# A chunked RWKV-7 scan in 64x64 cells: another order of the work on four engines within a period

## The reference, cut to what matters

```python
def step(s, inp):
    r_t, w_t, k_t, v_t, a_t, b_t = inp
    sa = jnp.einsum('bhij,bhj->bhi', s, a_t)
    s = s * w_t[:, :, None, :] + sa[..., None] * b_t[:, :, None, :] + v_t[..., None] * k_t[:, :, None, :]
    return s, jnp.einsum('bhij,bhj->bhi', s, r_t)
```

## Time and profile before

| what | value |
|---|---|
| median of 3 runs | 2223.35 us (2222.14 to 2228.94) |
| the profiled execution, own time | 2223.72 us |
| its span, first to last instruction | 2221.9 us |
| mean granted clock of TensorE | 0.982 |
| TensorE matmul busy | 2041.6 us, 92% |
| VectorE busy | 1130.4 us, 51% |
| ScalarE busy | 646.0 us, 29% |
| GpSimd busy | 539.7 us, 24% |
| DMA | 248.23 MB, 36.0% of 16 engines' time |

### The profile page before, as it was taken

The page is one execution under the profiler, slowest core; times in us unless marked ns, Lnnn a source line. Parts: engine busy times, 40 slices in busy tenths (PEclk is TensorE's granted clock), DMA queues, the critical chain, the costliest instruction groups (busy, mean ns, idle before and its releaser), DMA issues. The chain is left out here.

```text
span 2221.9 us, 64762 instructions
## 1 busy us (share of the span) xinstructions
PE 2041.6 (92%) x28556; PEld 1325.2 (60%) x28556; DVE 1130.4 (51%) x2187; ACT 646.0 (29%) x1825; POOL 539.7 (24%) x669
## 2 busy tenths in 40 slices
PE   7999999999999999999896888888988898889698
PEld 3556565355444455544344777787878787878443
DVE  5443343134946670042624665665666666656574
ACT  4111111134255532210012332333333333333332
POOL 1010010023032410011122333333433333333011
PEclk9999999999999999999997999999999999999899
DMA  9201002701127765555413233523333323232732
GB/s 354 81 20 38 19 19 107 291 29 38 32 76 205 192 174 182 176 165 190 144 64 109 72 95 97 141 71 94 80 84 82 90 75 94 73 91 61 235 119 109
DMA packets 269818, 248.23 MB, mean 112 GB/s; under 512 B 92769, under 2 KB 226145, under 8 KB 266082
## 3 DMA queue, kind: packets, MB, share of 16 engines
q1 hardware_dynamic: 269538, 244.09, 36.0%
HBM read 164.32 MB, written 79.69 MB: 110 GB/s over the span
## 5 line engine op out<-in xcount | busy, mean ns | idle before, releaser
L2168 PE MATMUL ps<-M,NG 64*64 64x64 f32 x6400 | 258.3, 222 | 44.0 <-DVE M L2046 42.7
L1019 PE MATMUL ps<-xt,w_slab 128*128 128x512 f32 (+1 forms) x800 | 297.5, 525 | 0.0
L2168 PEld LDWEIGHTS ps<-M,NG 64*64 64x64 f32 x6400 | 221.9, 136 | 60.8 <-DVE M L2046 54.3
L1019 PEld LDWEIGHTS ps<-xt,w_slab 128*128 128x128 f32 x800 | 148.3, 190 | 146.3 <-issue 122.6
L2168 PE MATMUL ps<-TT,MT 64*64 64x64 f32 x5120 | 209.9, 220 | 5.9 <-issue 3.4
L2168 PEld LDWEIGHTS ps<-TT,MT 64*64 64x64 f32 x5120 | 179.4, 135 | 16.4 <-issue 6.4
L1895 POOL TENSOR_TENSOR SP<-S,decay 128x128 f32<-128x128 f32 x152 | 61.2, 403 | 518.8 <-DVE S L2080 503.4
L2071 DVE STREAM_TRANSPOSE MT<-M 128x256 f32<-128x256 f32 x240 | 106.0, 442 | 147.9 <-ACT M L1958 147.9
L1958 ACT ACTIVATE M<-ps 128x128 f32<-128x128 f32 x240 | 66.6, 278 | 353.7 <-PE ps L2168 353.7
L2029 DVE COPY_PREDICATED TT<-mask,ps 128x128 f32<-128x128 int32 x400 | 123.5, 309 | 54.5 <-PE ps L2168 45.0
L645 PE MATMUL ps<-h,fgo 128*128 128x512 f32 x320 | 141.6, 597 | 2.4 <-PEq L202 2.4
(11 more groups left out here) (298 smaller groups left out, 3996.7 us busy)
## 6 DMA issues: line engine op xcount, KB each, us to landing
feat<-feature_scratch SPq DMA_DIRECT2D x160, 256.0 KB
feature_scratch<-k_feats SPq DMA_DIRECT2D x64, 320.0 KB, 5.2
feature_scratch<-k_feats SPq DMA_DIRECT2D x24, 640.0 KB, 6.9
k_feats<-in_modw SPq DMA_DIRECT2D x8, 1536.0 KB, 6.6
w_slab<-in_rwin SPq DMA_DIRECT2D x24, 512.0 KB, 6.7
V<-v_token_scratch SPq DMA_DIRECT2D x320, 32.0 KB, 2.6
fgo<-in_modw SPq DMA_DIRECT2D x8, 1024.0 KB, 9.2
fw_slab<-in_fwin SPq DMA_DIRECT2D x16, 512.0 KB, 4.5
```

The costliest lines, as they stand in the source:

```text
L1019: mm = pe.matmul(ps[:, bank, 0:n], (w1t if i is None else w[:, i % 2])[:, k, :], src[:, k, a:a + n], start=k == 0, stop=k == KT - 1)
L2168: mm = pe.matmul(out[o, b, :], L[o, b, :], R[o, b, :], start=True, stop=True)
```

## The change

The same instructions are issued in another order in the `period` functions of GpSimd, ScalarE, VectorE and TensorE. On GpSimd the product into `ar` slot 0 is taken out of `operands` as `last_operand`, and the second `state_scaled` of the period now stands between the two. On TensorE `products(0)` and `m4` stand between `a_state(0)` and `r_state(0)`, `products(1)` ahead of `b_state(0)`, `y(0)` behind `m8`, and `y(1)` behind `t32`. On ScalarE `r(0)`, `first_n(0)`, `m4` and `sa(0)` stand ahead of the exponentials, and `sa(1)` ahead of `m16`. On VectorE `first_x(1)` is moved behind the first mask and transpose and behind t2, and the table `DA` follows that order. SyncE's list is the same.

```diff
--- before.py
+++ after.py
@@ -1682,7 +1682,7 @@
 PB = {"m4": 1, "t8": 2, "m8": 3, "t16": 4, "m16": 5, "t32": 6, "mt32": 7}
 AA = {"n0": 1, "n1": 2, "m2": 3}
 AB = {"m4": 1, "m8": 2, "m16": 3, "xt": 4}
-DA = {"x0": 1, "x1": 2, "mt1": 3, "m1": 4, "t2": 5, "mt2": 6, "t4": 7}
+DA = {"x0": 1, "mt1": 2, "m1": 3, "t2": 4, "x1": 5, "mt2": 6, "t4": 7}
 DB = {"mt4": 1, "t8": 2, "mt8": 3, "t16": 4, "mt16": 5, "t32": 6}
 
 LAT_ONLY = lambda n: [0, 0] + [n] * (NCH - 2)
@@ -1903,19 +1903,26 @@
                 for slot, lo in ((0, 128), (1, 0)):
                     g.tensor_tensor(d4(bk[s][:, :, slot, :]), fe(every, lo, 768), d4(E3[s][:]), ALU.mult).then_inc(op_ready, 1)
                 chunk_done(g, j, cc - SETS)
-                g.tensor_tensor(d4(ar[l][:, :, 0, :]), fe(every, 384, 256), before(cc, every), ALU.mult).then_inc(op_ready, 1)
+                if is_lat(cc):
+                    g.tensor_tensor(d4(ar[l][:, :, 2, :]), fe(every, 512, 640), upto(cc, every), ALU.mult).then_inc(op_ready, 1)
                 g.tensor_tensor(d4(ar[l][:, :, 1, :]), d4(ident.unsqueeze(1).broadcast_to([P, B4, CK])),
                                 pend(cc, every).unsqueeze(3).broadcast_to([P, 2, 2, CK]), ALU.mult).then_inc(op_ready, 1)
-                if is_lat(cc):
-                    g.tensor_tensor(d4(ar[l][:, :, 2, :]), fe(every, 512, 640), upto(cc, every), ALU.mult).then_inc(op_ready, 1)
+
+            def last_operand(j, cc):
+                s, l = par(cc), lng(cc)
+                every = slice(0, P)
+                g.tensor_tensor(d4(ar[l][:, :, 0, :]), F[s][:, 384:896].rearrange("p (d x) -> p d x", d=2)[:, :, 0:P].rearrange("p d (b t) -> p d b t", b=2), before(cc, every), ALU.mult).then_inc(op_ready, 1)
 
             def period(j, c, ahead):
+                coming = ahead or c + 3 < NCH
                 if c >= 0:
                     state_scaled(j, c, 0)
-                    if c < NCH - 1:
-                        state_scaled(j, c, 1)
-                if ahead or c + 3 < NCH:
+                if coming:
                     operands(j, c + 3)
+                if 0 <= c < NCH - 1:
+                    state_scaled(j, c, 1)
+                if coming:
+                    last_operand(j, c + 3)
 
             for j in range(KT):
                 for c in range(0 if j else -3, NCH):
@@ -1973,30 +1980,29 @@
 
             def period(j, c, ahead):
                 A_, B_, Q_ = c + 2 >= 0 and (ahead or c + 2 < NCH), c + 1 >= 0 and (ahead or c + 1 < NCH), c >= 0
+                if Q_:
+                    r(j, c, 0)
+                if A_:
+                    first_n(j, c + 2, 0)
                 if B_:
                     second(j, c + 1, "m4")
                 if Q_:
-                    r(j, c, 0)
+                    sa(j, c, 0)
                 if ahead or c + 3 < NCH:
                     exps(j, c + 3)
                 if j == 0 and c == -2:
                     identities(1)
                 if A_:
-                    first_n(j, c + 2, 0)
-                if Q_:
-                    sa(j, c, 0)
+                    first_n(j, c + 2, 1)
                 if B_:
                     second(j, c + 1, "m8")
-                if A_:
-                    first_n(j, c + 2, 1)
                 if Q_ and is_lat(c):
                     y(j, c, 0)
                 if Q_:
                     r(j, c, 1)
+                    sa(j, c, 1)
                 if B_:
                     second(j, c + 1, "m16")
-                if Q_:
-                    sa(j, c, 1)
                 if A_:
                     first_m2(j, c + 2)
                 if Q_ and is_lat(c):
@@ -2085,37 +2091,34 @@
                     cums(j, c + 3)
                 if j == 0 and c == -2:
                     masks()
+                if A_:
+                    first_x(j, c + 2, 0)
+                if A_ and is_lat(c + 2):
+                    first_r(j, c + 2, 0)
                 if B_:
                     second_mt(j, c + 1, 4)
-                if A_:
-                    first_x(j, c + 2, 0)
-                    if is_lat(c + 2):
-                        first_r(j, c + 2, 0)
-                if B_:
                     second_t(j, c + 1, 8)
                 if Q_:
                     state(j, c, 0)
-                if B_:
-                    second_mt(j, c + 1, 8)
                 if A_:
-                    first_x(j, c + 2, 1)
                     first_mt1(j, c + 2)
                     first_m1(j, c + 2)
                 if B_:
+                    second_mt(j, c + 1, 8)
                     second_t(j, c + 1, 16)
                 if A_:
-                    if is_lat(c + 2):
-                        first_r(j, c + 2, 1)
                     first_t(j, c + 2, 2)
+                    first_x(j, c + 2, 1)
+                if B_:
+                    second_mt(j, c + 1, 16)
+                if A_ and is_lat(c + 2):
+                    first_r(j, c + 2, 1)
                 if Q_:
                     state(j, c, 1)
                 if B_:
-                    second_mt(j, c + 1, 16)
+                    second_t(j, c + 1, 32)
                 if A_:
                     first_mt2(j, c + 2)
-                if B_:
-                    second_t(j, c + 1, 32)
-                if A_:
                     first_t(j, c + 2, 4)
 
             for j in range(KT):
@@ -2314,23 +2317,23 @@
                 lat = Q_ and is_lat(c)
                 if Q_:
                     a_state(j, c, 0)
-                    r_state(j, c, 0)
+                if A_:
+                    products(j, a, 0)
                 if B_:
                     m4(j, b)
-                if A_:
-                    products(j, a, 0)
                 if Q_:
+                    r_state(j, c, 0)
                     sa(j, c, 0)
                 if B_:
                     t(j, b, 8)
+                if A_:
+                    products(j, a, 1)
                 if Q_:
                     b_state(j, c, 0)
+                if B_:
+                    m(j, b, 8)
                 if lat:
                     y(j, c, 0)
-                if B_:
-                    m(j, b, 8)
-                if A_:
-                    products(j, a, 1)
                 if Q_:
                     a_state(j, c, 1)
                     r_state(j, c, 1)
@@ -2344,12 +2347,12 @@
                     m(j, b, 16)
                 if Q_:
                     b_state(j, c, 1)
-                if lat:
-                    y(j, c, 1)
                 if A_:
                     m2(j, a)
                 if B_:
                     t(j, b, 32)
+                if lat:
+                    y(j, c, 1)
                 if A_:
                     t4(j, a)
                 if B_:
```

## The result

The changed kernel takes 2161.72 us (median of 4 runs, 2158.77 to 2175.07), the kernel before 2223.35 (median of 3, 2222.14 to 2228.94; a fourth execution, of 4065.29 us, was in the slower state and is left out): a ratio of 0.9728, 95% interval [0.9674, 0.9782]. Timed once more (v3_after) beside the kernel before it was 2163.72 against 2223.75, 0.9726 [0.9701, 0.9751]. The change gains 60 us, a third of the 181 forecast, and the time lies outside the stated range.

A forecast was written before the change was run, and what follows sets the result against it. The prediction took TensorE's stops from instruction order to bound the scan: 10.86 - 8.6 = 2.26 us saved per period, times 80 is 181 us, so 2223.7 - 181 = 2043 us, range 2019 to 2110.

The forecast's parts named there:

- The bound now: In the scan, TensorE's stops from the order of instructions, not an engine, take 2.24 us of each 10.86 us period.
- The schedule: Hand-laid latent period of TensorE, ScalarE and VectorE in the new order: one 0.13 us stop before t8, ending at 8.6 us.
- GpSimd: The second scaled state SP, behind four of five operand products, ends near 6.2 us, wanted at 7.45: 1.2 us of cover.
- Case 5: Rival: slower, since SP behind the operands delays the state sum if feature loads land late; 2288 us at 6 us; chance 0.03.
- SyncE: Its 8.38 us of issue per latent period fit the 8.6 us period with 0.2 us left.
- So 8.6 us: The hand-laid latent period of the scan, down from 10.86 us, saving 2.26 us in each of 80 periods.
- pure pace: Lower bound of the scan's period, TensorE's products summed without stops: 8.3 us, or 2019 us for the kernel.
- TensorE busy 97% or more: Sign that the forecast is right: TensorE busy at least 97% of the scan.
- Case 4: Rival: TensorE does not keep its pace without stops; only shown idle time, 1.31 us per period, goes: 2119 us; chance 0.06.

The follow-up runs named there:

- w5_stream: The changed kernel with two streams of 640 independent matmuls each behind its scan, the first without data transfers, the second beside 24 feature loads; 2251.03 us.
- x2_narrow: The changed kernel with products() issuing its 16 matmuls over 64 columns instead of 192 behind the first pair of heads, same instruction count; 2169.78 us, ratio 0.9744.
- x3_light: The changed kernel with every feature load behind the first four cut to 16 columns, the same DMAs; 2131.62 us, ratio 0.957.

## Why the prediction was right or wrong

**The bound now (right).** The stops were dependencies of the order, and the new order removed them: 47.6 us of idle time behind another engine in 500 before, 0.8 after.

**The schedule (right in its parts).** ScalarE's new order against the earlier trace rows: the SA copy stands ahead of the exponential, and in the second cell (1608.23) ahead of m16's copy (1610.57).

```profile
1603.67 0.28 ACT L1973 ACTIVATE SA<-ps 128x128 f32<-128x128 f32 x1 [0.19 <-PE ps L2292]
1603.84 0.41 ACT L1947 ACTIVATE decay<-cum 128x256 f32<-128x256 f32 x1
...
1608.23 0.28 ACT L1973 ACTIVATE SA<-ps 128x128 f32<-128x128 f32 x1 [0.66 <-PE ps L2292]
1610.57 0.28 ACT L1965 ACTIVATE M<-ps 128x128 f32<-128x128 f32 x1 [2.05 <-PE ps L2171]
```

VectorE's mask copy and transpose and the state sum against the earlier trace rows; the mask copy takes anything from 0.44 to 1.0 us in either kernel:

```profile
1606.65 0.45 DVE L2047 COPY_PREDICATED MT<-mask,NG 128x256 f32<-128x256 int32 x1
1607.13 0.45 DVE L2052 STREAM_TRANSPOSE M<-MT 128x256 f32<-128x256 f32 x1
...
1611.42 0.28 DVE L2086 TENSOR_TENSOR S<-ps,SP 128x128 f32<-128x128 f32 x1
```

The transpose ends at 1607.58, and t2 starts at 1608.00 where TensorE comes to it.

**GpSimd (right).** The operands, and the second SP behind them, against the earlier trace rows:

```profile
1604.63 1.40 POOL L1904 TENSOR_TENSOR bk<-feat,growth 128x256 f32<-128x256 f32 x2 [4.25 <-ACT growth L1949]
...
1606.81 0.51 POOL L1895 TENSOR_TENSOR SP<-S,decay 128x128 f32<-128x128 f32 x1 [0.20 <-DVE S L2086]
```

SP ends at 1607.32, four microseconds ahead of the state sum at 1611.42. Case 5 did not happen.

**SyncE (right that it would fit, for the wrong reason).** Against the earlier trace rows:

```profile
1612.28 2.54 SPq L1857 DMA_DIRECT2D y_scratch<-Y  x4
...
1617.76 3.28 SPq L1848 DMA_DIRECT2D V<-v_token_scratch  x4
1621.92 0.59 SPq L1857 DMA_DIRECT2D y_scratch<-Y  x1
```

It issues from 1612.28 to 1621.04, 8.76 us, and the next store is at 1621.92. In an 8.6 us period it would have been over its time. It never came to that, and no run tests it.

**"So 8.6 us", and with it the bound of 8.3 us from "pure pace" (wrong).** This is the step that failed. The pace was read from stretches of 16 to 48 matmul records, and summed to a period as if TensorE could hold it over 640 instructions. It cannot: a block of 256 takes 3.9 us in the quiet and about 4.2 in this scan, where the summed pace needs 8.6 x 256 / 640 = 3.4. With 624 instructions a period in the mean, 2.43 blocks, the rates of w5_stream put the period between 2.43 x 3.9 = 9.5 and 2.43 x 4.6 = 11.2 us (an estimate), and 10.20 was measured at a DMA share between those of the two streams. The pace between stops was right: with 59.6 us of issue idle and 76 such stops in 49 periods, each stop with its 0.16 us of drain, 1.22 + 0.25 = 1.47 us of the 1.60 between 8.6 and 10.20 are stops for instructions. So the sign "TensorE busy 97% or more" did not show (88.8 of 100 us). The saving is 80 x (10.86 - 10.20) = 53 us in the profiled run, the slowest of the four, and 60 in the medians.

**The rivals.** Case 4 had the right kind, TensorE not keeping its pace when no stop lets instructions pile up, at a chance of 0.06, with a price from the shown idle time (2119 us) that has nothing to do with the mechanism and is still 43 us too low. The row that points to the price could be read from the trace of the kernel before: queue q8, kind instruction, 192 packets in the scan. It would not have told the limit, since the old order asked for a block only in 4.47 us, but it would have told that the forecast asked for one in 3.5.

The Trainium skill, page "Runtime: NRT & Kernel Launch", section "Instruction fetch mechanics", says that an engine's instructions are refilled in 16 KiB blocks of 256 while the last block is executed, and that crossing a block's end is "mostly hidden". The block size agrees with the packets here (16.4 KB, 256 instructions). That the cost is hidden does not: 59.6 of 500 us in the changed kernel. Its other rule, in "TensorE: Matmul & The Clock Gate", section "Wait — 56ns, not 53.3ns?", of starts at least 25 ns apart, stays contradicted by the products of four quadrants, as in sa with 16 records in 0.28 us, 17.5 ns each.

That the limit is the fetch of instructions from memory is shown by the packets' size and count, by stops inside products that have no wait, and above all by the time at which each stop ends, 1.2 to 1.7 us behind a packet. That the width of the matmuls does not matter to it is shown by x2_narrow and w5_stream. That data transfers lengthen a block rests on x3_light (4.17 to 3.94 us) and on the two streams (3.9 to 4.6). What makes a block with many semaphore waits slower was not found.

## What to carry to other kernels

Count instructions beside time. For small float32 matmuls (four TensorE instructions each), divide the count of a period, semaphore instructions included, by 256 and multiply by 3.9 to 4.6 us as the DMA engines are idle or half busy; if a new order would go below that, the gain stops there, and the next step is fewer instructions, not a better order. When idle time is put down to "issue" and stands inside a product, look at the instruction queue's row, and at when its packets land, before any semaphore.

A schedule laid from short stretches is trustworthy for where stops go, and says nothing on what the engine can hold up for a whole period.

## What the runs showed of the hardware that was not expected

- A block of 256 TensorE instructions: 3.9 us with the DMA engines quiet, 4.6 us at a DMA share of 0.46, 3.94 to 4.2 in the scan, 4.5 to 4.7 in the scan with 30 semaphore instructions more a period.
- TensorE's stops for instructions end 1.2 to 1.7 us behind the end of an instruction packet, in 70 of 70 of the changed kernel.
- A wait on TensorE that is already satisfied can be an instruction of its own and fills the blocks: 2400 more gave 201 packets for 192, and cost 110 us in the new order and 77 in the old: 10 to 14 ns each by themselves, the larger part as waiting for instructions.
- Eight float32 matmuls of 8 columns hold TensorE as long as eight of 64: 16 records in 0.48 us.
- A products() of 4 matmuls with 128 output partitions each took 0.85 us, the one of 8 matmuls on four quadrants 0.70.
